# Gate rows of two attention parts by way of DRAM instead of matmuls with the identity

## The reference, cut to what matters

```
mod = (silu_c @ ada_w[i] + ada_b[i])[:, None, :]
sh1, sc1, g1, sh2, sc2, g2 = jnp.split(mod, 6, axis=-1)
h = x * (1.0 + sc1) + sh1
y = mixer(h)
x = layer_norm(DN_ALPHA * x + g1 * y, ln_g[i, 0], ln_b[i, 0])
```

## Time and profile before

| | us |
|---|---|
| median of 3 runs | 2629.72 (2628.79 to 2630.74) |
| the profiled execution, its own time | 2631.81 |
| its span in the trace | 2630.0 |
| TensorE busy | 2578.3 (98%) |
| VectorE busy | 2005.4 (76%) |
| ScalarE busy | 602.5 (23%) |
| GpSimd busy | 117.3 (4%) |

### The profile page before, as it was taken

The page is one execution under the profiler, slowest core; times in us unless marked ns, Lnnn a source line. Parts: engine busy times, 40 slices in busy tenths (PEclk is TensorE's granted clock), DMA queues, the critical chain, the costliest instruction groups (busy, mean ns, idle before and its releaser), DMA issues.

```text
span 2630.0 us, 31829 instructions
## 1 busy us (share of the span) xinstructions
PE 2578.3 (98%) x13052; PEld 2115.3 (80%) x13052; DVE 2005.4 (76%) x2304; ACT 602.5 (23%) x1284; POOL 117.3 (4%) x95
## 2 busy tenths in 40 slices
PE   6999999999999999999999999999999999999999
PEld 3788888888877876899788888788888888878887
DVE  4788786978658747887876888787687778978776
ACT  2112121311221137222210332410021023242101
POOL 0000000000000012200000002010000000100000
PEclk8999999999999999999999999999999999999999
DMA  7543342444543633555554545355555555444653
GB/s 272 176 139 102 98 143 75 140 154 160 176 160 129 214 75 79 183 192 167 194 184 162 191 160 192 113 194 184 177 192 180 188 175 186 144 145 160 200 183 121
DMA packets 252577, 424.54 MB, mean 161 GB/s; under 512 B 35584, under 2 KB 93376, under 8 KB 251920
## 3 DMA queue, kind: packets, MB, share of 16 engines
q1 hardware_dynamic: 248352, 410.09, 47.5%
q0 software_dynamic: 2560, 7.16, 0.9%
q10 hardware_dynamic: 1520, 5.25, 0.5%
HBM read 419.32 MB, written 3.15 MB: 161 GB/s over the span
## 4 chain that ended last, share of the span: by engine, by line
PE 90%; DVE 5%; ACT 3%; issue 1%; DMA 1%; ACTq 0%; POOL 0%; DVEq 0%
PE psum L504 85%; PE psum L518 2%; DVE wgt_lo L1771 1%; PE psum L839 1%; DVE wgt_hi L1769 1%; DMA raw<-ada_w 1%; ACT xh L1216 1%; ACT W L1216 0%; ACT L1216 0%; DVE xl L1792 0%; DVE W L2256 0%; ACT n_prob_b L1216 0%; PE psum L662 0%; DVE xl L1780 0%; DMA cst<-consts 0%
## 5 line engine op out<-in xcount | busy, mean ns | idle before, releaser
L1771 DVE TENSOR_TENSOR wgt_lo<-raw,wgt_hi 128x2048 fp32r<-128x2048 f32 (+1 forms) x336 | 761.9, 2268 | 11.5
L504 PE MATMUL psum<-wgt_hi,xh 128*128 128x512 f32 (+1 forms) x1744 | 683.8, 392 | 2.8 <-DVE wgt_lo L1771 1.4
L504 PE MATMUL psum<-wgt_hi,xl 128*128 128x512 f32 (+1 forms) x1744 | 677.4, 388 | 0.0
L504 PE MATMUL psum<-wgt_lo,xh 128*128 128x512 f32 (+1 forms) x1728 | 670.7, 388 | 0.0
L1769 DVE CAST wgt_hi<-raw 128x2048 fp32r<-128x2048 f32 (+1 forms) x336 | 408.4, 1216 | 127.3 <-PE psum L504 119.5
L504 PEld LDWEIGHTS psum<-wgt_hi,xh 128*128 128x128 f32 x1744 | 328.2, 188 | 72.7 <-issue 6.4
L504 PEld LDWEIGHTS psum<-wgt_hi,xl 128*128 128x128 f32 x1744 | 327.9, 188 | 66.6
L504 PEld LDWEIGHTS psum<-wgt_lo,xh 128*128 128x128 f32 x1728 | 325.4, 188 | 62.5
L504 PE MATMUL psum<-wgt_hi,yh 128*128 128x512 f32 x928 | 365.3, 394 | 1.4 <-DVE wgt_lo L1771 1.0
L504 PE MATMUL psum<-wgt_hi,yl 128*128 128x512 f32 x928 | 362.0, 390 | 0.0
L504 PE MATMUL psum<-wgt_lo,yh 128*128 128x512 f32 x928 | 361.8, 390 | 0.0
(11 more groups left out here) (238 smaller groups left out, 2189.3 us busy)
## 6 DMA issues: line engine op xcount, KB each, us to landing
raw<-mlp_w SPq DMA_DIRECT2D x64, 1024.0 KB, 5.4
raw<-w_in SPq DMA_DIRECT2D x60, 1024.0 KB, 4.8
raw<-ada_w SPq DMA_DIRECT2D x48, 1024.0 KB, 5.3
raw<-ffn_w_gate SPq DMA_DIRECT2D x40, 1024.0 KB, 5.1
raw<-ffn_w_up SPq DMA_DIRECT2D x40, 1024.0 KB, 5.0
raw<-ffn_w_down SPq DMA_DIRECT2D x40, 1024.0 KB, 5.0
raw<-ret_w_in SPq DMA_DIRECT2D x24, 1024.0 KB, 5.1
raw<-nat_w_in SPq DMA_DIRECT2D x12, 1024.0 KB, 5.2
```

The source lines that it names most:

```text
L504: return pe.matmul(o, l, r, start=start_, stop=stop, skip_group_check=True)
L1771: v.tensor_tensor(wgt_lo[:, s % RING, :size], r, wgt_hi[:, s % RING, :size], ALU.subtract).then_inc(split_done.sem, split_done.up())
```

## The change

The two calls of `gates` for part 2 are taken out, on TensorE and on ScalarE. In their place ScalarE stores the columns of the gate to a DRAM tensor, element by element, one DMA for each stream: for layer 0 behind the Silu of head 0, where it had copied the gates; for layer 1 behind the first two exponentials of the attention. GpSimd waits for the stores and loads each row back with one DMA that repeats it over the 128 partitions: for layer 0 behind its power for head 0, for layer 1 when all 32 pairs of scores are computed, since the place is taken until then. `add_gated` waits for these loads where the gate's part is 2.

```diff
+        gate_stored = signal("gate_stored", 16)
+        gate_in = signal("gate_in", 16)
...
+        gate_store = [nc.dram_tensor(f"gate_store{i}", (2 - i, D), F32, kind="Internal").ap() for i in range(2)]
...
@@ TensorE
-                if h == 0:
-                    gates(0, 2, 2)
                 pe.wait_ge(out_of(("ro", h, 2)), emptied(("ro", h, 2)))
...
-            gates(1, 2, 1)
             tokens_by_features("ny", ...
...
@@ ScalarE
+            def store_gate(layer, streams):
+                act.wait_ge(out_of(("mod", layer, 2)), emptied(("mod", layer, 2)))
+                for st in range(streams):
+                    act.dma_start(gate_store[layer][st].rearrange("(k p) -> p k", p=P),
+                                  mod[:, layer, 2, :, st], allow_slow_non_contiguous=True).then_inc(gate_stored.sem, gate_stored.up())
...
                 if h == 0:
-                    gates(0, 2, 2)
+                    store_gate(0, 2)
...
             nat_exp(0)
             nat_exp(1)
+            store_gate(1, 1)
...
-            gates(1, 2, 1)
             gates(1, 5, 1)
@@ VectorE, add_gated
-                dve.wait_ge(out_of(gate), emptied(gate))
+                if gate[2] == 2:
+                    dve.wait_ge(gate_in.sem, gate_in.at(32 if gate[1] == 0 else 48))
+                else:
+                    dve.wait_ge(out_of(gate), emptied(gate))
@@ GpSimd
+            def load_gate(layer, streams):
+                pool.wait_ge(gate_stored.sem, gate_stored.next(streams))
+                for st in range(streams):
+                    pool.dma_start(gate_of(layer, 2, st), gate_store[layer][st:st + 1, :].to_broadcast([P, D])).then_inc(gate_in.sem, gate_in.up())
+
             for h in range(RET_HEADS):
                 rstd(small[:, 88:92], small[:, 92:96], 4, rstd_dve)
+                if h == 0:
+                    load_gate(0, 2)
...
             for b in range(1, KT):
                 add_window(b)
+            pool.wait_ge(scores_full.sem, scores_full.at(N_PAIRS))
+            load_gate(1, 1)
             ln_table(1, 0)
```

## The result

| | before | after |
|---|---|---|
| median of 19 runs each, us | 2630.43 | 2634.8 (2632.85 to 2637.93) |
| ratio of the times, 95% interval | | 1.0017 (1.0011 to 1.0024) |
| span of the profiled execution, us | 2630.0 | 2633.9 |
| TensorE busy, us | 2578.3 | 2576.0 |

What follows compares the result with a forecast made beforehand. TensorE, busy for 98% of the span, was taken as the bound. Removal -3.23, issue +0.1 and layer 1 -1.65 summed to -4.8 us, giving 2625.0 us from the median 2629.72, range 2623.3 to 2629.3.

Steps and rivals of the forecast that it cites:

- Place 1, the round trip: Layer 0, head 0: stores land at 132.5 us, gate back at 139.9, 1.9 us ahead of VectorE's need.
- the broadcasts: Layer 0, head 0: GpSimd's two loads to all partitions land in 6.5 us, at most 9.7.
- late case: Layer 0, head 0: with both upper ends the gate lands at 149.2 us and costs 5.1; total 2630.0.
- The price of a late gate: Layer 0, head 0: VectorE's 2.3 us lead absorbs lateness until 144.1; each further microsecond is one of TensorE's.
- Rival 1: Layer 0, head 0: gates come back late from DRAM, costing 5.1 us with both upper ends, total 2630.0; chance 0.08.
- within 0.2%: Whole kernel: measured time would differ from before by no more than 0.2%, 5.3 us; chance 0.71.
- Place 1, the removal: Layer 0, behind head 0: removing the gate matmuls saves 5.78 - 2.55 = 3.23 us, not their full 3.73.
- Place 1, the issue on ScalarE: Layer 0, head 0: issuing two stores behind the last Silu delays the copies ry waits for; charged 0.1 us.
- Rival 2: Layer 0, head 0: store issue on ScalarE delays ry by up to 2.6 us, total 2627.5; chance 0.15.
- Place 2: Layer 1, behind the attention: removing the gate matmuls lets ny start earlier; 1.71 us goes, taken as 1.65.
- The sum: Both places together: -3.23 + 0.1 - 1.65 = -4.8 us, forecast 2625.0 us.
- Rivals 3 and 4: Both places. Third: matmul time counts in full, 5.4 us saved, chance 0.10. Fourth: VectorE limits instead, 2629, chance 0.07.

Runs made afterwards that it cites:

- packed store: Against the changed kernel, each store is 128 runs of 32 bytes instead of 1,024 of 4 bytes, gate values returning in another order; measured 2625.65 us, ratio 0.9982.
- the early one: Against the changed kernel, layer 0's two stores are issued ahead of head 0's Silus instead of behind them; measured 2625.76 us, ratio 0.9984.

## Why the prediction was wrong

**Place 1, the round trip: this step failed.** I took 4.2 us for the stores' landing, and 10.3 as the upper end. It was 12.7. The value came from the store of 1 MB, because it was the only store to DRAM by ScalarE's queue; the nearest row by shape, `nat_rpb` with its many short runs, had given the upper end, and both are transfers whose pieces share nothing on the writing side. I had weighed the number of pieces by them, and the number costs 1 us. That neighbouring elements are written as separate pieces side by side in DRAM had no row, and in the sum I had priced it at nothing, though I had quoted the Trainium skill for it: "DMA: Bandwidth & Descriptors" says in its table of specifications that pieces below 512 B are read, modified and written. The packed store (32-byte pieces, 1.9 us) and the pieces with 64 bytes of their own (3.1 us) are both below 512 B and quick, so the size alone didn't make a store slow here; and no view shows whether anything was read and modified. That page's section "Rules for kernel authors" says that a strided last dimension becomes one descriptor for each element. The number of pieces that follows from it costs 1 us of the 12 here.

The second term of the same step, the broadcasts, was taken at 6.5 us with 9.7 as its upper end, and took 9.2. I had them in a time in which SP asks for nothing, although by my own shift of 3.1 us SP's load of 139.95 would come at 136.9 and meet their end; in the packed kernel it came at 136.03, and they took 4.7. Being late, they met SP's weight loads, the first of which was issued at 137.41 and itself held up. In the table by stretch it moved 2 GB/s from 138 to 140 us and 81 GB/s from 140 to 142, in the kernel after:

```profile
138.00:140.00 2.00, 2.00 (x10) 1.68 (x9) 1.97 (x2) 0.00 (x0) 0.00 (x0) 1.00 0.08 2
140.00:142.00 2.00, 2.00 (x10) 1.65 (x10) 2.00 (x2) 0.00 (x0) 0.29 (x1) 1.00 0.61 81
```

Before, a load issued at 139.95 moved 290 GB/s from 141 to 143. So 127.9 + 0.4 + 12.7 + 0.9 + 9.2 = 151.1, by the form of my late case; the gated product started at 151.72.

**The price of a late gate: the form was right, and a term was missing.** I had said that VectorE's lead of 2.3 us swallows the first part of a wait and the rest is TensorE's. 9.23 - 2.3 = 6.9; TensorE's stretch from `ry` to the next `rs` grew by 9.92. The remaining 3.0 us are the half clock behind the idle time, for which I had no term, in the sum or in the rivals. Four stretches of 2 us at 0.50, 0.50, 0.50 and 0.78, less where TensorE was not yet working, give 0.5 x 5.35 + 0.22 x 2 = 3.1, which agrees.

**Rival 1 is what happened.** I gave it 0.08, of which 0.05 for a total slower by over 0.2%, and forecast 2630.0 for its late case. Its first point of decision was right: the kernel is slower once the gate lands behind 149. The second, 2635 only behind 154, was not: it landed at 151.6 and the median is 2634.8, since the clock's 3 us were missing. (The 4.3 us that it sets against 144.1 are 4.2 by its own terms.) Its chance was too small, since I took two upper ends from rows of another kind as if they bounded the store, while I wrote myself that no row has such a store. A cost that nothing bounds from above, on the only path with four handovers, should have had a chance near that of the forecast. I had also called "within 0.2%" the likely outcome (0.71), and +0.17% lies within it. That is luck: it lies on the other side of no change, and comes from a loss of 9.92 us that I did not expect, set against two gains that I did.

**Place 1, the removal: right.** Forecast 3.23, measured 2.97 together with the next step, for which I had charged 0.1.

**Place 1, the issue on ScalarE: right.** The two issues took 1.03 us together, beside the Silu. The copies begin 1.08 us behind the Silu's start instead of 0.49, and `ry` is 0.26 us later than in the forecast's 2.55. Rival 2 (2627.5) is out: the step costs 0.3 and not 2.6. Its upper end, twice 1.55 us, was drawn too low: other windows of `nat_rpb` took up to 2.92 to issue in the same trace.

**Place 2: right.** Forecast 1.65, measured 1.79, and nothing in layer 1 waits for the gate. The store landed after 11.3 us and the load after 4.1, with all the time that they had. The start of `ny` against the last transposes:

```profile
1051.72 0.44 PE L863 MATMUL psum<-cst,W 128*128 128x128 f32 x2
...
1051.91 0.48 PE L508 MATMUL psum<-wgt_hi,yh 128*128 128x512 f32 x1
```

**The sum.** With the round trip in time it holds, in two kernels: the packed store gave -4.7 us by the ratio and the early one -4.2, against -4.8. Rivals 3 and 4 (5.4 us and 0.8 us) lie on either side of these, and the two intervals (-2.4 to -7.1 and -1.8 to -6.3) leave out the fourth but not the third, against which the trace speaks: 2.97 + 1.79 = 4.76 and not 5.44.

## What to carry to other kernels

Before moving work off a busy engine on to a path through DRAM, count the time that each handover has, and treat a transfer of a kind that no row shows as having no upper bound: issue it as early as its data allows, which here cost nothing and turned +4.4 us into -4.2. Don't write single elements side by side into DRAM; pack what one partition holds into one run, and keep such a store away from loads that others wait for. Elements 64 bytes or more apart landed quickly too. Neither is a finished recipe: the packed values came back in another order, which a real kernel has to undo, and reading the spread ones back wasn't run. The kernel with the early stores needs neither. Only take instructions off the bound engine where the wait that would take their place is shorter than they are, and count a wait of several microseconds on TensorE with the slow clock behind it.

## What the runs showed of the hardware

- A store of 1,024 elements of 4 bytes (4 KB), side by side in DRAM, landed after 9.6 to 13.0 us; the same elements 64 to 512 bytes apart after 2.5 to 4.1 us at head 0 and 6.4 to 6.6 in layer 1; 128 runs of 32 bytes after 1.9 (median) and 4.7. At head 0 of the changed kernel the packets were over within 3 us of the issue; in the early-store kernel, behind a weight load, they ran from 106 to 108 us with the issue at 103.0.
- While such a store was out, other transfers slowed down: an issue on SP took 8.68 us, where the longest of its kind before took 2.92, and two weight loads landed after 9.4 us, against 5.0 with the packed store (medians). The first of them moved 2 GB/s and then 81 GB/s from 138 to 142 us, where one before reached 290.
- Behind 6.30 us without matmuls TensorE came back at the level of 1.2 GHz, for some 6 us more, which cost 3.0 us. Behind 2.00 us at the same place it came back at 2.4 GHz, and behind the norm's 1.9 us at either level, from trace to trace.
